# First stage of a hybrid SSD and Hyena block on one core: tile groups, transposes and projection slabs in another order

## The reference, cut to what matters

```python
sh1, sc1, ... = adaln(c, ada_w, ada_b, 6)         # silu(c) @ ada_w + ada_b
csh1, csc1 = adaln(c_ctx, ada_w, ada_b, 2)
hx = modulate(rmsnorm(x, norm1_g), sh1, sc1)      # h * (1 + scale) + shift
hc = modulate(rmsnorm(ctx, norm1_g), csh1, csc1)
p  = hx @ w_in                                    # here: its first 512 xbc columns,
                                                  # and the 64 dt columns
h  = sin(freq1 * (feats @ w1 + b1))               # first layers of the Hyena filters
h  = sin(freq2 * (h @ w2 + b2))
```

## Time and profile before

| | us |
|---|---|
| three runs | 2340.36, 2343.83, 2344.83; median 2343.83 |
| the profiled execution | 2344.3, of it 2342.7 span from the first to the last instruction |
| PE busy | 2195.3 (94%), its weight loads 1756.0 (75%) |
| DVE, ACT, POOL busy | 1531.3, 1044.5, 107.1 |
| mean granted clock of TensorE | 0.974 |

### The profile page before, as it was taken

How to read it: one execution, slowest core, us unless ns; L and a number is a source line. 1 busy time by engine, 2 the same in 40 slices (tenths; PEclk the granted TensorE clock), 3 DMA queues, 4 the chain that set the end, 5 groups by cost and what they waited for, 6 DMA issues and landing times. The chain is left out here.

```text
span 2342.7 us, 31655 instructions
## 1 busy us (share of the span) xinstructions
PE 2195.3 (94%) x11986; PEld 1756.0 (75%) x11986; DVE 1531.3 (65%) x2081; ACT 1044.5 (45%) x1347; POOL 107.1 (5%) x120
## 2 busy tenths in 40 slices
PE   5989998998999999999999999996899999999995
PEld 1568886544899877777778999985688888778784
DVE  2256566765564577877775445554677777899897
ACT  2324333121564433333333334443655555677774
POOL 1000000000000002020201100000000000000000
PEclk9989999998999999999999999997999999999997
DMA  8862334998667644344433556743478888999993
GB/s 309 312 216 84 99 84 168 380 374 332 187 189 218 185 131 130 113 134 124 143 120 109 151 169 181 238 149 108 142 258 288 274 280 268 316 347 387 353 362 137
DMA packets 309786, 500.62 MB, mean 214 GB/s; under 512 B 16710, under 2 KB 160673, under 8 KB 308247
## 3 DMA queue, kind: packets, MB, share of 16 engines
q1 hardware_dynamic: 304870, 481.02, 62.0%
q0 software_dynamic: 4784, 17.83, 2.3%
HBM read 496.65 MB, written 2.13 MB: 213 GB/s over the span
## 5 line engine op out<-in xcount | busy, mean ns | idle before, releaser
L187 DVE TENSOR_TENSOR w_lo<-raw,w_hi 128x1024 fp32r<-128x1024 f32 x712 | 865.7, 1239 | 477.7 <-ACT w_hi L183 460.1
L183 ACT ACTIVATE w_hi<-raw 128x1024 fp32r<-128x1024 f32 x712 | 744.1, 1059 | 684.0 <-PE bank L195 511.3
L193 PE MATMUL bank<-h,w_hi 128*128 128x256 f32 (+1 forms) x896 | 296.3, 331 | 11.0 <-DVE w_lo L187 4.3
L194 PE MATMUL bank<-h,w_hi 128*128 128x256 f32 (+1 forms) x896 | 291.8, 326 | 0.0
L195 PE MATMUL bank<-h,w_lo 128*128 128x256 f32 (+1 forms) x896 | 291.4, 325 | 0.0
L1490 PE MATMUL bank<-h,w_hi 128*128 128x512 f32 x768 | 276.4, 404 | 0.0
L1492 PE MATMUL bank<-h,w_lo 128*128 128x256 f32 x768 | 216.2, 282 | 0.0
L193 PEld LDWEIGHTS bank<-h,w_hi 128*128 128x128 f32 x896 | 173.6, 194 | 33.8 <-issue 12.9
L195 PEld LDWEIGHTS bank<-h,w_lo 128*128 128x128 f32 x896 | 173.7, 194 | 13.5
L194 PEld LDWEIGHTS bank<-h,w_hi 128*128 128x128 f32 x896 | 173.7, 194 | 12.7 <-issue 0.5
L1490 PEld LDWEIGHTS bank<-h,w_hi 128*128 128x128 f32 x768 | 145.5, 189 | 37.8 <-issue 3.7
(11 more groups left out here) (430 smaller groups left out, 3610.6 us busy)
## 6 DMA issues: line engine op xcount, KB each, us to landing
raw<-in_w_in SPq DMA_DIRECT2D x240, 512.0 KB, 4.4
raw<-in_ada_w SPq DMA_DIRECT2D x192, 512.0 KB, 5.8
raw<-in_moe_w_gate SPq DMA_DIRECT2D x128, 512.0 KB, 4.9
raw<-in_moe_w_up SPq DMA_DIRECT2D x128, 512.0 KB, 5.8
raw<-in_moe_w_down SPq DMA_DIRECT2D x128, 512.0 KB, 6.1
raw<-in_w_ssd_out SPq DMA_DIRECT2D x32, 512.0 KB, 4.8
raw<-in_w_hy_out SPq DMA_DIRECT2D x32, 512.0 KB, 3.4
raw<-in_w_o SPq DMA_DIRECT2D x32, 512.0 KB, 4.6
```

What stands on the lines that cost most here:

```text
L183: act.activation(self.k.w_hi[:, j % HL, :], self.k.raw[:, j % RAW, :], ACT.Copy).then_inc(self.hi_ready, 1)
L187: dve.tensor_tensor(self.k.w_lo[:, j % HL, :], self.k.raw[:, j % RAW, :], self.k.w_hi[:, j % HL, :].bitcast(F32), ALU.subtract).then_inc(s ...
L193: pe.matmul(out, lhs[0], rhs[0], start=start, stop=False)
L194: pe.matmul(out, lhs[0], rhs[1], start=False, stop=False)
```

## The change

The groups become 2, 4, 4, 4, 2 tiles, so the narrow groups are the first and the last. The projection slabs stand in the middle of a group's slabs in the load order: behind 8, 6, 6, 6, 4 of them. PE begins the transposes behind four slabs of group 0, in runs of four row tiles. The waits on the tokens are split in two: `x` by `in_tok`, `ctx` by a new semaphore `in_ctx`. Group slabs on PE now stand in fours (or other even numbers), the second filter layer moves to behind project(2), `columns(4)` to ahead of project(13), and ACT and DVE split the projection slabs behind a group's h tiles instead of ahead of the next group's.

```diff
-        TILES1 = (4, 4, 4, 2, 2)
-        FIRST1 = (0, 4, 8, 12, 14)
+        TILES1 = (2, 4, 4, 4, 2)
+        FIRST1 = (0, 2, 6, 10, 14)
...
-        order1 = [(MOD, 0, j) for j in range(slabs_of(0))]
-        for g in range(1, LAST1 + 1):
-            for m in range(2 * g - 2, 2 * g):
-                order1.append((PROJ, m, 0))
-            order1 += [(MOD, g, j) for j in range(slabs_of(g))]
+        PROJ_OF = ((0,), (1, 2), (3, 4), (5, 6), (7,))
+        PROJ_AT = (8, 6, 6, 6, 4)
+        order1 = []
+        for g in range(LAST1 + 1):
+            order1 += [(MOD, g, j) for j in range(PROJ_AT[g])]
+            order1 += [(PROJ, m, 0) for m in PROJ_OF[g]]
+            order1 += [(MOD, g, j) for j in range(PROJ_AT[g], slabs_of(g))]
...
-                mods(0, 0, 12)
+                mods(0, 0, 4)
+                pe.wait_ge(s.norm, 4)
+                for kt in range(4):
+                    tokens(kt)
+                mods(0, 4, 6)
+                for kt in range(4, 8):
+                    tokens(kt)
+                mods(0, 6, 8)
...
-                mods(0, 12, 16)
-                mods(1, 0, 1)
-                pe.wait_ge(s.norm, 4)
-                for j in range(8):
-                    tokens(2 * j)
-                    tokens(2 * j + 1)
-                    mods(1, j + 1, j + 2)
+                for kt in range(8, 12):
+                    tokens(kt)
+                mods(1, 0, 2)
+                for kt in range(12, 16):
+                    tokens(kt)
                 columns(0)
-                mods(1, 9, 13)
+                mods(1, 2, 6)
...
                 project(0)
-                mods(1, 13, 16)
+                mods(1, 6, 12)
+                mods(1, 12, 16)
                 project(1)
...
+                second_layer()
+                for g in (2, 3):
+                    first = FIRST1[g]
+                    for n in range(3):
+                        mods(g, 4 * n + 4, 4 * n + 8)
+                        project(first - 3 + n)
+                    columns(g)
+                    mods(g + 1, 0, 4 if g == 2 else 2)
+                    project(first)
+                mods(4, 2, 4)
                 project(11)
-                mods(4, 2, 6)
+                mods(4, 4, 8)
                 project(12)
-                mods(4, 6, 8)
+                columns(4)
                 project(13)
-                columns(4)
                 project(14)
                 project(15)
...
-                act.wait_ge(s.in_tok, 32)
+                act.wait_ge(s.in_tok, 16)
                 for t in range(4):
+                    if t == 2:
+                        act.wait_ge(s.in_ctx, 16)
...
+                    if g < LAST1:
+                        for m in PROJ_OF[g + 1]:
+                            slab_high(m)
```

More of the change, by code:

```diff
@@ L307, in build @@
         (s.in_rows, s.in_c, s.in_tok, s.in_small, s.colT, s.cols, s.cact, s.raw_used, s.mrow, s.mT, s.mod, s.act, s.h1mm, s.h1arg, s.hm, s.tokT, s.xt, s.fulls, s.hi, s.lo, s.norm,
-         s.wdt, s.dt_hi, s.dt_lo) = sems(
+         s.wdt, s.dt_hi, s.dt_lo, s.in_ctx) = sems(
             "p1", "in_rows", "in_c", "in_tok", "in_small", "colT", "cols", "cact", "raw_used", "mrow", "mT", "mod", "act",
-            "h1mm", "h1arg", "hm", "tokT", "xt", "fulls", "hi", "lo", "norm", "wdt", "dt_hi", "dt_lo")
+            "h1mm", "h1arg", "hm", "tokT", "xt", "fulls", "hi", "lo", "norm", "wdt", "dt_hi", "dt_lo", "in_ctx")
         AHEAD = 3
         k.steps_done = sem("p1_steps_done")
-        TILES1 = (4, 4, 4, 2, 2)
-        FIRST1 = (0, 4, 8, 12, 14)
+        TILES1 = (2, 4, 4, 4, 2)
+        FIRST1 = (0, 2, 6, 10, 14)
         LAST1 = len(TILES1) - 1
@@ L379, in _ @@
                 pool.dma_start(toks[:, TT:2 * TT, :],
-                               io["ctx"][0].rearrange("(t p) d -> p t d", p=P)).then_inc(s.in_tok, 16)
+                               io["ctx"][0].rearrange("(t p) d -> p t d", p=P)).then_inc(s.in_ctx, 16)
                 pool.dma_start(feats[:], consts["feats"]).then_inc(s.in_small, 16)
@@ L452, in project, with second_layer @@
                         mm.then_inc(k.steps_done, 1)
-                mods(0, 0, 12)
+                def second_layer():
+                    pe.wait_ge(s.hm, 1)
+                    pe.wait_ge(s.mod, 3)
+                    for half in range(2):
+                        rows_ = slice(half * FILT, (half + 1) * FILT)
+                        mm = pe.matmul(k.psum[7][rows_, 256:512], fw2[rows_, :], k.hmid[rows_, :], start=True, stop=True)
+                    mm.then_inc(s.h1mm, 1)
+                mods(0, 0, 4)
[6 more added lines that the diff above has]
+                mods(0, 6, 8)
                 pe.wait_ge(s.in_rows, 16 * n_rows_dma)
@@ L477, in _ @@
                 project(0)
-                mods(1, 13, 16)
+                mods(1, 6, 12)
+                mods(1, 12, 16)
                 project(1)
-                mods(2, 0, 1)
                 columns(1)
+                mods(2, 0, 4)
                 project(2)
[L483 to L504, removed]
+                second_layer()
[8 more added lines that the diff above has]
+                mods(4, 2, 4)
                 project(11)
-                mods(4, 2, 6)
+                mods(4, 4, 8)
                 project(12)
-                mods(4, 6, 8)
+                columns(4)
                 project(13)
-                columns(4)
                 project(14)
@@ L549, in _ @@
                                    ACT.Copy).then_inc(s.xt, 1)
-                    if kt in (1, 3):
-                        slab_high(kt // 2)
+                    if kt == 7:
+                        slab_high(0)
                 act.wait_ge(s.xt, KT)
                 for g in range(LAST1 + 1):
-                    if 0 < g < LAST1:
-                        slab_high(2 * g)
-                        slab_high(2 * g + 1)
+                    highs(g)
                     if g in (0, 3):
@@ L560, in _ @@
                         act.activation(k.hmid[:], farg[:, 0, :], ACT.Sin).then_inc(s.hm, 1)
-                    highs(g)
+                    if g < LAST1:
+                        for m in PROJ_OF[g + 1]:
+                            slab_high(m)
                 for j in range(AHEAD):
@@ L620, in _ @@
                 slab_low(0)
-                slab_low(1)
                 bias = k.vcol[:, VEC_AT["ada_b"]:VEC_AT["ada_b"] + 2 * KT].rearrange("p (h kt) -> p h kt", h=2)
@@ L658, in _ @@
                         sine_argument(k.psum[7][:, 256:512], 2, 3)
-                    if 0 < g < LAST1:
-                        slab_low(2 * g)
-                        slab_low(2 * g + 1)
                     mod_columns(g)
@@ L668, in _ @@
                     if g < LAST1:
+                        for m in PROJ_OF[g + 1]:
+                            slab_low(m)
                         mod_rows(g + 1)
```

## The result

| | before | changed |
|---|---|---|
| five runs each, median, us | 2343.83 | 2325.14 |
| lowest and highest | 2340.36, 2350.31 | 2320.15, 2329.29 |
| profiled execution, us | 2344.3 | 2329.3 |
| end of the first stage in its trace, us | 166.3 | 148.6 |

The ratio of the changed kernel to the one before is 0.992, with a 95% interval of 0.9905 to 0.9934: 18.7 us faster. The forecast was 2325.

A forecast was written before the change was run, and what follows sets the result against it. Slab supply bounds the stage's first half, PE the second: 62.2 us to the last group 1 slab, plus 78.9 PE work, 3.3 waits and 2.9 clock, ends at 147.3; 19.0 saved gives 2325 us, range 2318 to 2334.

The forecast's parts named there:

- The total: Whole kernel: first stage ends at 147.3 us instead of 166.3, gaining 19.0, so 2325 us.
- First group, narrow slabs: Loads at the start: eight narrow slabs at 1.48 us instead of 1.35 land 1.1 us later.
- Tokens: Transposes start near 31 us; their 8.7 us hide under PE's waits for slabs, up to 62 us.
- project(0): First projection on PE: reached at 48.7 us, ended at 52.1, covered by PE's waiting.
- The supply: Slab loads: one every 1.36 us without a stop, so group 1's last slab, number 26, lands at 62.2 us.
- list of held slots: SP queue: slabs 15, 16, 33, 34, 51, 52 hold projection-slab slots; 23, 41, 59 wait for them; tight, no loss.
- PE's own sum from there: PE after 62.2 us: slabs, projections, columns and second layer total 78.9 us, reaching 141.1.
- Waits on DVE: PE around columns(1) to (4): waits of 0.7, 0.3, 0.7 and 1.6, sum 3.3 us; none behind columns(4).
- Clock: Two old dips, 4.6 and 1.4 us, go; one new dip behind columns(3), 0 to 4.6, taken as 2.9.
- Rival 1: Transposes: clock stays low until about 50 us, losing 4.7, time 2330; chance 0.16 including late token rows or fourth slab.
- Rival 3: SP queue at slabs 23, 41, 59: unsplit projection slabs block loads, 28.2 us added, time 2353; chance 0.04.

The follow-up runs named there:

- late_tokens: Changed kernel with the transposes put back behind all of group 0's slabs, two row tiles per slab of group 1: stage end 166.1 us, median 2341.24 us, ratio 0.9997.
- one_token_wait: Changed kernel with ACT's squares waiting for x and ctx together, as before: stage end 149.6 us, median 2327.09 us, ratio 0.9945.
- late_tokens_free: late_tokens with projection slabs 1 and 2 split while the tokens are still copied: stage end 153.8 us, median 2334.61 us, ratio 0.9967.
- dve_order: Changed kernel with DVE copying group 0's rows and splitting projection slab 0 before the dt split and sine argument: stage end 147.8 us, median 2325.47 us.
- odd_counts: Changed kernel with slabs of groups 2 and 3 taken 5, 3, 5, 3 at a time instead of fours: stage end 148.4 us, median 2326.26 us.
- dve_four: dve_order with four narrow slabs instead of two between columns(3) and project(10): stage end 143.6 us, median 2323.82 us, ratio 0.9925.
- proj_front: Changed kernel with each later group's two projection slabs loaded ahead of its slabs instead of in their middle: stage end 169.6 us, median 2346.92 us, ratio 1.0016.
- after_again: The changed kernel run and profiled once more, unaltered: stage end 150.0 us, median 2324.77 us, ratio 0.9915.

## Why the prediction was right, and where not

*The total* came out as said: 2325.14 against 2325. That it came so close is luck, in two places. The stage was said to end at 147.3 and ended at 148.6, because three errors nearly cancel: project(1) began 3.2 us later than by the sum (66.4 against 63.2), PE's sum from there was 1.0 longer, and a dip of 2.9 that was counted did not come in this profile. And the stage gave 17.7 us, not 19.0; the medians differ by 18.7, within their scatter. The mechanism, transposes moved under the wait for slabs, is what the trace shows. These are the steps.

*First group, narrow slabs.* Said: 1.1 us later. Not so: in late_tokens, where PE takes all eight at once, the last one starts at 34.01, as before (34.16). What changed is the queue: it issued slab 8 at 33.11 instead of 28.23, which the text did not name; the narrow slabs took it 9.4 us more to issue.

*Tokens.* Right: start near 31 (30.01), hidden under the waits. That a delay of up to 5 us is absorbed is not borne out: of some 4 us about half was (one_token_wait). And the price if they are late was wrong. The text had 8.7 us of PE time; it was 14.9 at project(1), of which 10.1 came through the held slots (late_tokens_free).

*project(0).* Said 48.7, seen 51.92. The step that failed is the list of what PE waits for: the copy of group 0's rows behind DVE's dt split and sine argument, 2.64 us, and the low clock behind it: sixteen transposes in 3.4 us instead of 2.0. dve_order removed both; in one_token_wait the same 2.64 us had no low clock behind it (1.97 us for the block at 48.85), so the second is not the sure price of the first.

*The supply.* Slab 26 said to land at 62.2; PE ended it at 66.4, of which 3.3 went with dve_order, where PE took it at 62.07. The prediction's list of held slots leaves out slab 8, projection slab 0, whose slot slab 16 waits for: 6.6 us, the longest of the queue's waits, until DVE had split it at 45.3.

*PE's own sum from there.* Said 78.9 + 3.3 = 82.2 from the last slab's arrival, or 81.2 from its product's end; seen 148.6 - 66.4 = 82.2. The sum was right to 1 us, in part by luck: the wide slabs took 18.1 us instead of 15.7, since PE waited for some of them inside the blocks, and projections and columns 1.1 less than priced. Its premise was half right: odd_counts shows that PE's time was not the only bound, since 3.2 us of extra work moved nothing. The text said the two ran level, and they did.

*Waits on DVE.* Said 0.7, 0.3, 0.7, 1.6; seen 0.72, 0.23, 0.72, 1.58.

*Clock.* Said one dip of 2.9 behind columns(3). It is there in five of the nine profiles with the 1.6 us wait, with 1.6 to 2.9 us; what brings it is open (dve_four). And the dip at the old end cost 1.6, not 1.4: two projections in a row are 6.4 us, not 6.8. In the changed kernel's profile other dips stood in its place, at 44 to 48 and 62 to 65 us.

*Rival 1,* a low clock through all the transposes, did not come: the second and the third sixteen took 1.97 us each at full clock (35.24 and 39.27 in the changed kernel's timeline are such blocks; the first, 3.67 us at 30.01, was slow, and so were the first of the slabs behind it, 1.70 at 33.61). The last sixteen, 3.43 us at 44.87, were slow too, behind the wait of 2.64. The rule of the Trainium skill (TensorE: Matmul & The Clock Gate, Part 4) is neither shown nor excluded, since slabs stand between all blocks; as a forecast of this kernel's time it would have been wrong by 5 us.

*Rival 3,* held slots, was rightly small for the change as made, and it is the mechanism on which the change rests: proj_front puts it in, and the time is above the kernel before.

## What to carry to other kernels

In a ring that is refilled in order, ask of every slot who gives it back and what that one waits for; a consumer two engines away that stands behind late work can cost more than the work itself, here 10 of 15 us. Undo parts of a change one at a time before crediting them: the new grouping looked like its core, and a kernel without it has a stage 8 us shorter. And put ready work into waits of 1.6 us and more on TensorE: in five of nine profiles the lower clock behind such a wait cost as much again as the wait, or more.

## What the runs showed of the hardware

Eight loads of narrow slabs (1 KB runs, 512 KB each) took the queue 24.9 us to issue at the start where eight with 2 KB runs took 15.5, though PE had the last of them at the same time (34.01 in late_tokens, 34.16 before). The low clock behind the same wait of 1.6 us comes in some executions and not in others of one program (125.14 against 125.01 above), and it came behind columns(2) with waits of only 0.2 to 0.3 us near it (98.94 in after_again). Sixteen transposes in a row ran at the full clock, 1.97 us, with four-strip slab products between the blocks. In the first 34 us the granted clock reads 1.00 while products take twice their later time (3.67 us against 1.97 for sixteen transposes).
